# Two transformer blocks on one core: the constants and one modulation product per layer fetched at other places, and 64 columns instead of 128 in the last attention's value products

## The reference, cut to what matters

```
for i in range(2):                                    # first block
    h = 0.5 * swiglu(x, ffn1...)                      # 1024 -> 2752 -> 1024
    x = layer_norm(ALPHA * x + h, ln_g[i, 0], ln_b[i, 0])
    h = hybrid_mixer(x, w_in[i], ...) # NSA (compressed, selected, window), differential, forgetting attention
    x = layer_norm(ALPHA * x + h, ln_g[i, 1], ln_b[i, 1])
    h = 0.5 * swiglu(x, ffn2...)
    x = layer_norm(ALPHA * x + h, ln_g[i, 2], ln_b[i, 2])
    x = x + sigmoid(x @ ple_w_gate[i] + b) * (p[i] @ ple_w_proj[i])
for i in range(2):                                    # second block, also on 256 context tokens
    m = silu(c) @ ada_w[i] + ada_b[i]                 # 9 shifts, scales and gates of 1024; the same for c_ctx
    x = x + 0.5 * gt1 * swiglu_2(modulate(x, ...))
    y = conformer_conv(...) if i == 0 else windowed_gqa_sink(...)
    x = x + gt2 * y
    x = x + 0.5 * gt3 * swiglu_2(modulate(x, ...))
return rmsnorm(x, final_g)
```

## Time and profile before

| | |
|---|---|
| median of 3 runs | 3120.54 us (3120.41 to 3131.64) |
| the profiled execution | 3129.2 us |
| its span, first to last instruction | 3127.4 us |
| PE busy | 2965.4 us (95%) |
| DVE, ACT, POOL busy | 1637.2, 1291.8, 167.0 us |
| chain of waits | PE 82%, DVE 12% |
| mean granted clock of PE | 0.975 |
| moved from and to memory | 443.10 MB |

### The profile page before, as it was taken

How to read it: one execution, slowest core, us unless ns; L and a number is a source line. 1 busy time by engine, 2 the same in 40 slices (tenths; PEclk the granted TensorE clock), 3 DMA queues, 4 the chain that set the end, 5 groups by cost and what they waited for, 6 DMA issues and landing times.

```text
span 3127.4 us, 51125 instructions
## 1 busy us (share of the span) xinstructions
PE 2965.4 (95%) x17586; PEld 2533.1 (81%) x17586; DVE 1637.2 (52%) x3043; ACT 1291.8 (41%) x2519; POOL 167.0 (5%) x121
## 2 busy tenths in 40 slices
PE   7999899999998999999999878999999999989998
PEld 7978789799797897788886545788878888768998
DVE  5565765555647656533335796433335333448554
ACT  4444445455544455432332444323324323335553
POOL 0000010000010100000000670000000000000000
PEclk9999899999998999999999988999999999989999
DMA  7555265555652656533333762333314233241553
GB/s 256 184 163 199 72 202 178 174 183 182 181 161 69 220 179 177 172 108 95 104 97 114 256 223 81 121 95 96 105 54 139 92 106 98 81 143 50 175 181 98
DMA packets 239052, 443.10 MB, mean 142 GB/s; under 512 B 26400, under 2 KB 27424, under 8 KB 238240
## 3 DMA queue, kind: packets, MB, share of 16 engines
q1 hardware_dynamic: 237344, 432.94, 44.1%
q0 software_dynamic: 1536, 7.86, 0.8%
HBM read 439.65 MB, written 1.05 MB: 141 GB/s over the span
## 4 chain that ended last, share of the span: by engine, by line
PE 82%; DVE 12%; issue 2%; POOL 2%; ACT 1%; DMA 1%; SPq 0%; DVEq 0%; POOLq 0%; ACTq 0%
PE ps L736 81%; DVE low L1720 1%; DVE hidden L1723 1%; POOL hidden L2306 1%; DVE zl L1723 1%; DMA raw<-weights 1%; DVE ps L1723 1%; DVE hidden L1720 1%; DVE zl L1720 1%; DVE coef L2228 1%; DVE hidden L2232 1%; POOL low L2276 1%; DVE gated L1720 1%; DVE hidden L2055 0%; DVE neg_max L2028 0%
## 5 line engine op out<-in xcount | busy, mean ns | idle before, releaser
L736 PE MATMUL ps<-zh,low 128*128 128x256 f32 (+1 forms) x4192 | 1400.6, 334 | 79.1 <-DVE low L1720 41.1
L736 PE MATMUL ps<-zl,high 128*128 128x256 f32 (+1 forms) x4192 | 1381.8, 330 | 0.0
L736 PE MATMUL ps<-zh,high 128*128 128x256 f32 (+1 forms) x4192 | 1380.9, 329 | 0.0
L1720 DVE TENSOR_TENSOR low<-raw,high 128x512 fp32r<-128x512 f32 x1276 | 843.8, 699 | 462.1 <-ACT high L1277 460.3
L1277 ACT ACTIVATE high<-raw 128x512 fp32r<-128x512 f32 x1304 | 761.7, 625 | 572.6 <-PE ps L736 499.5
L736 PEld LDWEIGHTS ps<-zh,low 128*128 128x128 f32 x4192 | 806.0, 192 | 184.0 <-DVE low L1720 42.2
L736 PEld LDWEIGHTS ps<-zl,high 128*128 128x128 f32 x4192 | 806.7, 192 | 71.8 <-issue 4.8
L736 PEld LDWEIGHTS ps<-zh,high 128*128 128x128 f32 x4192 | 806.5, 192 | 69.1
L1720 DVE TENSOR_TENSOR hidden<-gated,ps 128x256 f32 (+1 forms) x176 | 91.5, 520 | 604.2 <-ACT gated L1277 604.2
L1277 ACT ACTIVATE gated<-ps 128x256 f32<-128x256 f32 (+1 forms) x176 | 81.3, 462 | 497.3 <-PE ps L736 497.1
L736 PE MATMUL ps<-high,zl 128*128 128x512 f32 (+2 forms) x544 | 195.2, 359 | 3.8 <-DVE zl L1720 3.8
(11 more groups left out here) (190 smaller groups left out, 2016.8 us busy)
## 6 DMA issues: line engine op xcount, KB each, us to landing
raw<-weights SPq DMA_DIRECT2D x1640, 256.0 KB, 3.4
hidden<-norms POOLq DMA_DIRECT2D x4, 1024.0 KB, 7.0
cst<-consts SPq DMA_DIRECT2D x1, 1829.0 KB, 14.3
x<-x_in SPq DMA_DIRECT2D x1, 1024.0 KB, 7.0
x<-tokens_in POOLq DMA_DIRECT2D x1, 1024.0 KB, 13.8
x<-ctx_in POOLq DMA_DIRECT2D x1, 1024.0 KB, 6.4
out<-hidden POOLq DMA_DIRECT2D x1, 1024.0 KB, 5.1
ple_p<-p_in POOLq DMA_DIRECT2D x1, 512.0 KB, 7.2
```

The source lines that it names most:

```text
L736: return nc.tensor.matmul(out, lhsT, rhs, start=first, stop=last, **kw)
L1720: return nc.vector.tensor_tensor(out, a, b, op)
```

## The change

1. SP issues the constants behind quarter 7 instead of behind quarter 1.
2. In both mixers of the first block, the fill that stood in the normalization behind the mixer (`eps` 1) now stands between the scores of the compressed keys and the wait for their softmax, with banks 3 and 4 for rows and columns. In the stream it follows the phi weights' fill directly. `post_norm` keeps its fill where `eps` is 0. PE checks in `jobs`, before the first use of banks 3 and 4 there, that the fill's rows and columns were taken.
3. In the last attention the products with values take their 64 columns once.

```
@@ stream
         yield ("phi2", l, 0, 2, True)
         yield fills.pop()
+        yield fills.pop()
         yield from (("rows", ("w_out", l), t, 2, False) for t in range(KT - 2))
         yield ("rows", ("w_out", l), KT - 2, 4, False)
-        yield fills.pop()
@@ SP
-            load(0, weights[0])
-            load(1, weights[1])
-            sp.dma_start(cst[:], consts).then_inc(consts_landed, 16)
-            for n in range(2, RING):
+            for n in range(RING):
                 load(n, weights[n])
+                if n == 7:
+                    sp.dma_start(cst[:], consts).then_inc(consts_landed, 16)
@@ PE post_norm, and the same on ACT
-                self.fill(2, 3)
+                if eps == 0:
+                    self.fill(2, 3)
@@ PE mixer
                 m.then_inc(cmp_scores, 1)
+                self.fill(3, 4)
                 pe.wait_ge(cmp_probs, seen(cmp_probs))
@@ PE jobs
                 for j in range(n + 3):
+                    if j == 2:
+                        self.fills_out()
...
-                            o = self.mm(ps[:, 5 + a % 2, m * P:m * P + P], probs_t[:, a % 2, i * P:i * P + P],
-                                        v_of(a, kb, v).unsqueeze(1).broadcast_to([P, 2, 64]), kb == 0, kb == kbs(a) - 1)
+                            va = v_of(a, kb, v) if maps == 1 else v_of(a, kb, v).unsqueeze(1).broadcast_to([P, 2, 64])
+                            o = self.mm(ps[:, 5 + a % 2, m * P:m * P + (64 if maps == 1 else P)], probs_t[:, a % 2, i * P:i * P + P],
+                                        va, kb == 0, kb == kbs(a) - 1)
@@ DVE post_norm
-                pending = self.taken < self.fills
-                self.filled()
+                pending = eps == 0 and self.taken < self.fills
+                if eps == 0:
+                    self.filled()
```

## The result

| | before | with the change |
|---|---|---|
| median | 3125.02 us | 3136.05 us |
| lowest and highest run | 3119.51 to 3131.64 (12 runs) | 3128.83 to 3154.67 (12 runs) |
| the profiled execution, its span | 3129.2, 3127.4 us | 3128.83, 3127.0 us |
| PE busy | 2965.4 us | 2958.4 us |
| mean granted clock of PE | 0.975 | 0.974 |

The ratio is 1.0035, with a 95% interval of [1.0022, 1.0048]. The change makes the kernel 7 to 15 us slower, under the 0.5% that the prediction called no change. Its median lies 1 us above the range given; before had its median at 3125.02 in these runs, 4.5 above the 3120.54 that the sum started from.

A forecast was written before the change was run, and what follows sets the result against it. TensorE (PE), busy for 95% of the span, was taken as the bound. From 3120.5 us, -4.5 + 2 x 4.0 - 2 x 1.0 + 0 = +1.5 gave 3122.0 us, with a range of 3107 to 3135.

The forecast's parts named there:

- Start, -4.5: Kernel start: quarters 2 to 7 pass the constants, so PE runs on earlier; -4.5 us, between -1 and -4.7.
- The cover named for the constants: Kernel start: PE's eight quarters of work, until 26 at least, cover the constants' later landing and splitting, done at 24.3.
- Mixer, +4.0 each: Compression step, both mixers: w_out's quarters, fetched late behind the fill, delay DVE and the jobs; +4.0 us each.
- the two estimates: Mixer: w_out's three quarters, issued from about 318.7, reach ACT at 326.5 to 328.0, or land at 325.4 to 326.7.
- 4.1 to 5.3 late: Mixer: the first row maximum starts at 328.7 to 330 where it began at 324.67, delaying PE's second pair of jobs.
- Normalization, -1.0 each: Behind both mixers: DVE starts 3.2 us later, yet about a microsecond is gained; -1.0 us each.
- PE waits for the same low half: Normalization behind the mixer: POOL holds up DVE's low halves as before, so PE meets the same gate wherever it stood.
- Last attention, 0: Last attention: halving product columns gains nothing, as weights set the time and DVE has hardly any idle; between -3.5 and 0.
- (2): Last attention: columns count, halving 0.12 us on 256 passes; 15.4 us faster, 3106.6 us; chance 0.05.
- (4): Last attention: the clock falls to half, +2.1 us on 16 pairs of jobs, 3155.6 us; chance 0.03.
- (3): Mixers: two fills in a row need five quarters more than the ring holds; at worst 3135.4 us; chance 0.18.
- (1): Mixers: the fill fits PE's wait and the clock returns earlier, -2.5 us a mixer; 3109 us; chance 0.16.

The follow-up runs named there:

- e3: The kernel before with only the constants issued behind quarter 7: 3120.42 us, ratio 0.9976.
- e8: The changed kernel with four feed-forward quarters split ahead of the normalization behind the mixer instead of eight: 3131.37 us, ratio 1.0013.
- e1: The kernel before with only the 64 columns in the last attention's value products: 3128.29 us, ratio 0.9997.
- e7: The kernel before with the split of the output product's first three quarters moved behind the jobs: 3125.8 us, ratio 0.9996.
- e10: The kernel before with constants behind quarter 7 and the output product's first three quarters split behind the jobs, fill unmoved: 3123.1 us, ratio 0.9983.
- e2: The changed kernel with 128 columns in the last attention's value products again: 3137.68 us, ratio 1.0034.
- e5: The kernel before with only the moved fill: 3143.58 us, ratio 1.0047.
- e15: The changed kernel, unrepaired, with 1, 2 and 1 idle products in three PE waits ahead of the compressed scores: 3135.81 us, ratio 1.0027.
- e9: The changed kernel with two repairs: w_out's first three quarters split behind the jobs, four feed-forward quarters ahead of the normalization: 3116.15 us, ratio 0.9975.
- e14: e9 with 1, 2 and 1 idle products in the three PE waits ahead of the compressed scores: 3114.39 us, ratio 0.9958.
- e12: e10 with 2, 3, 2 and 5 idle products in four PE waits of the compression step: 3114.66 us, ratio 0.9947.
- e13: e9 with 2, 3 and 2 idle products in the three PE waits ahead of the compressed scores: 3108.68 us, ratio 0.9937.

## Why the prediction failed by a little

**Start, -4.5 (bounds -1 to -4.7): right.** Measured -4.5 in the first stage, and -4 to -11 us by e3. The cover named for the constants held: ACT waited 3.75 us for them and no product of PE did.

**Mixer, +4.0 each (bounds -2.5 to +6.5): this is the step that failed, by size.** The mechanism is the one given: w_out's quarters come as the sixth to eighth of a burst, and DVE's low halves in front of the heads carry the delay to the jobs. But it costs +6.7 and +6.3 in the stage, near the upper bound. Three terms in it were short. First, the turned rows were priced at 0.95 us, from a row at the full clock, though the sentence beside it says that the clock is low here; they took 1.86, and the fill 3.64 for 3.4, so the transposes came 2.82 us late for "2 us late". Second, the burst starts later: its first issue was put at 318.7, and in before's time it came at 315.70 + (314.95 - 310.12) = 320.5. Of these 1.8 us, 0.7 are the turned rows. The rest is the time from the fill's first product to the first issue, 1.94 us (313.76 to 315.70) where the sum has 0.85. Even the model for it, the second fill before, was read early: its slots were said to come free at 375.2, and SP's first issue behind that fill stands at 376.08. From the issue on, the first of w_out's quarters landed 7.2 us later, inside the 6.7 to 7.8 of the two estimates. The first maximum was thus 1.1 us beyond the later end of "4.1 to 5.3 late". Third, the half microsecond credited to the clock, which brought the term down to 4.0, was not earned: the lower level lasted 23.9 us in both traces of the first mixer, and in the second 27.3 us for 23.9. SP's row in the trace before, behind the second fill:

```profile
376.08 14.51 SPq L674 DMA_DIRECT2D raw<-weights  x24
```

**Normalization, -1.0 each (bounds -3.5 to +3.2): right in size, half right in its path.** The 3.2 us by which DVE starts late are there (e8 gives 31.9 - 28.7 = 3.2; the stretch is 27.1 in the first layer of before and e3, but 28.7 in that of e1, e7 and e10, which don't touch this place either), and PE starts transposing later. But "PE waits for the same low half" was wrong: with eight quarters split ahead, PE had products enough to pass POOL's operations without a wait, and the norms landed 5.5 us behind their issue, not 7. From the jobs' end over both stretches, the four kernels with the fill ahead of the jobs and all eight quarters split (after, e2, e5, e15) have 226.1, 226.3, 227.8 and 226.2 us in the second layer, the five with the fill in the normalization (before, e1, e3, e7, e10) 230.6, 228.1, 226.8, 228.4 and 229.6: 2.1 us between the means. In the first layer the means differ by 0.2, the other way. So about -1 each, but the layers don't agree, and single traces scatter by more than that; that the mean meets the forecast is in part luck.

**Last attention, 0: right.** e1 and e2 show nothing, jobs stay at 2.03 us, and the clock was 1.00; rivals (2) and (4) fell. In the profiled execution of e1 the mean clock was 0.97 between 2820 and 2870 and the jobs took 62.3 us. That is no fall within the jobs: the lower level began ahead of them, at 2795.7, and ended at 2823.0, and in e2, with 128 columns, it lasted from 2797.3 to 2821.2 (jobs 61.2 us; before and after 60.2). Whether transposes count toward the clock, no run here separates.

**The sum.** With the measured terms: -4.5 + 6.7 + 6.3 - 2 = +6.5 us. The interval is +7 to +15, and the medians differ by 11.0. So of the 14 us between the forecast 3122.0 and 3136.05, 4.5 are the median of before (3125.02 for 3120.54), 5.0 the two mixers, and about 4.5 stay open. They go with the fill: e5 costs 15.7 us by the medians, where its terms give 6.7 + 6.3 - 2 = 11.0. The traces don't show them. The runs of the changed kernel reach 3154.67 at a mean clock of 0.963, where its shortest has 0.974. The clock as a cause of that spread rests on the clocks of the runs and on e9 and e14, not on a trace of such a run.

**Rivals.** (3), the fetch burst, was named as slower, and it is the mechanism that was at work, in my own term and beyond it: its threshold, w_out's third quarter later than 322, was passed by more than 5 us: the first of the three landed at 322.92, which is 327.8 in before's time. Its worst case, 3135.4, is close to the measured time by luck: its 13 us for the mixers were there, its 6.4 us for the normalizations were not. (1), holes filled for nothing, fell for the changed kernel; in e9's first mixer the clock came back with the fill, after the ring's wait was gone.

## What to carry to other kernels

Work moved into a wait of one engine takes its transfers with it: before filling a hole, count which slots of the ring the moved transfers take, what is fetched behind them, and who on every other engine stands in line behind that. Price work in the stretch where it will stand, with that stretch's granted clock, and not by the row of the place it comes from. Where a path depends on the clock, a kernel needs several runs before a few microseconds are read. A wait removed may pay twice, once for itself and once by the clock behind it.

## What the runs showed of the hardware

- The same instructions in the same execution took 59.6 us at a mean granted clock of 0.80 and 50.5 us at 1.00 (e14). With products that nobody reads in waits of 1.2 to 2.5 us ahead of these jobs, the level was 1.00 over the jobs of all four profiled mixers of e12 and e13. They made the kernel with the repairs 12 us faster by the ratios (0.9975 to 0.9937), although they outlasted the waits. With fewer of them (e14) it fell again in one mixer of two.
- A burst of eight 256 KB quarters was issued within 3.65 us, and the sixth took 4.95 us from issue to landing, where the median over the kernel is 3.4 us.
- A float32 product of 512 columns with 32 columns of weights took 0.94 us when all went to one strip (e12), and 0.24 us when they rotated over four.
- In the last attention, with a weight load of 128 columns for each pass, eight float32 passes took 1.06 us with 128 columns of data and 1.00 to 1.10 us with 64.
